# A hybrid DeltaNet and RG-LRU backbone on one core: another formula, buffers and engine split in the RG-LRU scan stage, and layer 1 in column order

## The reference

```python
h_lat = rmsnorm(x, norm_g[i]) * (1.0 + scale[:, None]) + shift[:, None]
if col_major:
    h_lat = to_col_major(h_lat, rows)
...
xb, gate = jnp.split(h @ w_in, [LRU_W], axis=-1)
xc = short_conv(xb, conv_w) + conv_b
r = jax.nn.sigmoid(einsum(xblk, w_r) + b_r)          # per direction, 4 blocks of 256
i = jax.nn.sigmoid(einsum(xblk, w_i) + b_i)
log_a = -RG_C * r * jax.nn.softplus(-lam)
a = jnp.exp(log_a)
b = jnp.sqrt(-jnp.expm1(2.0 * log_a)) * (i * xc)
h_t = a_t * h_{t-1} + b_t                            # forward and backward, from the context's state
y = ((h_f + h_b) * jax.nn.silu(gate)) @ w_out
...
x = x + gate[:, None] * from_col_major(y); return rmsnorm(x, final_g)
```

## Time and profile before

| | us |
|---|---|
| median of 3 runs (4928.4 to 4930.95) | 4929.32 |
| the profiled execution | 4928.78 |
| its span in the trace | 4927.0 |
| norm of layer 1 | 3806 to 3895 |
| projection of layer 1 | to 4304 |
| scan stage: first loads, last product | 4309 to 4727.0 |
| output stage | 4731 to 4927 |

### The profile page before, as it was taken

The page is one execution under the profiler, slowest core; times in us unless marked ns, Lnnn a source line. Parts: engine busy times, 40 slices in busy tenths (PEclk is TensorE's granted clock), DMA queues, the critical chain, the costliest instruction groups (busy, mean ns, idle before and its releaser), DMA issues. The chain is left out here.

```text
span 4927.0 us, 83385 instructions
## 1 busy us (share of the span) xinstructions
PE 4166.3 (85%) x30756; PEld 3449.3 (70%) x30756; DVE 2875.9 (58%) x3373; ACT 2115.1 (43%) x3991; POOL 1906.6 (39%) x1256
## 2 busy tenths in 40 slices
PE   7599999999997888888888888876998599956559
PEld 2378888888885777777777777765887488745447
DVE  3244545454544777777777777765543633268864
ACT  4122222223222666666666666642111611167732
POOL 2212112121211776666666676643110522123222
PEclk8799999999998999999999999997999699978779
DMA  6212221222122444444444444335443221221234
GB/s 230 84 48 78 66 80 54 82 66 77 53 84 75 114 112 114 111 115 114 111 113 111 116 113 114 109 99 197 174 187 118 72 82 57 73 79 62 79 128 141
DMA packets 589103, 503.79 MB, mean 102 GB/s; under 512 B 115585, under 2 KB 557185, under 8 KB 575873
## 3 DMA queue, kind: packets, MB, share of 16 engines
q1 hardware_dynamic: 588960, 501.82, 33.2%
HBM read 351.00 MB, written 150.67 MB: 102 GB/s over the span
## 5 line engine op out<-in xcount | busy, mean ns | idle before, releaser
L551 PE MATMUL pj_bank<-h_hi,pj_whi 128*128 128x512 f32 (+1 forms) x1920 | 717.7, 374 | 22.5 <-POOL pj_wlo L537 19.2
L551 PE MATMUL pj_bank<-h_lo,pj_whi 128*128 128x512 f32 (+1 forms) x1920 | 708.1, 369 | 0.0
L551 PE MATMUL pj_bank<-h_hi,pj_wlo 128*128 128x512 f32 (+1 forms) x1920 | 707.9, 369 | 0.0
L741 ACT ACTIVATE pj_raw<-pj_bank 128x512 f32<-128x512 f32 (+1 forms) x240 | 128.1, 554 | 956.4 <-PE pj_bank L551 477.5
L534 POOL TENSOR_TENSOR pj_whi<-pj_w,ones 128x1024 fp32r<-128x1024 f32 x48 | 115.3, 2403 | 1025.4 <-PE pj_bank L551 1010.9
L551 PEld LDWEIGHTS pj_bank<-h_hi,pj_whi 128*128 128x128 f32 x1920 | 363.3, 189 | 88.1 <-POOL pj_wlo L537 19.6
L1364 DVE TENSOR_TENSOR dc_Y<-dc_psY,dc_pick 128x256 f16<-128x256 f32 x864 | 322.4, 413 | 167.8 <-PE dc_psY L1115 167.8
L1270 ACT ACTIVATE dc_R<-dc_psR 128x256 f16<-128x256 f32 x720 | 245.5, 382 | 394.5 <-PE dc_psR L1131 393.6
L551 PEld LDWEIGHTS pj_bank<-h_lo,pj_whi 128*128 128x128 f32 x1920 | 363.5, 189 | 62.5 <-issue 3.8
L551 PEld LDWEIGHTS pj_bank<-h_hi,pj_wlo 128*128 128x128 f32 x1920 | 363.0, 189 | 61.1
L834 DVE TENSOR_SCALAR pj_acc<-pj_raw,pj_conv_w 128x2307 f32<-128x2307 f32 x32 | 90.7, 2834 | 475.2 <-ACT pj_raw L741 475.2
(11 more groups left out here) (273 smaller groups left out, 10778.2 us busy)
## 6 DMA issues: line engine op xcount, KB each, us to landing
dc_tm<-scratch_tm SPq DMA_DIRECT2D x288, 192.0 KB, 2.4
dc_cgr<-scratch_cgrow SPq DMA_DIRECT2D x288, 128.0 KB, 2.8
dc_fm<-scratch_fm SPq DMA_DIRECT2D x288, 128.0 KB, 2.3
scratch_o<-dc_ob SPq DMA_DIRECT2D x288, 128.0 KB, 2.0
scratch_tm<-pj_tm SPq DMA_DIRECT2D x24, 1152.0 KB, 5.2
pj_w<-in_gdn_w_in SPq DMA_DIRECT2D x48, 512.0 KB, 6.3
scratch_fm<-pj_row SPq DMA_DIRECT2D x16, 1152.0 KB, 5.2
dc_kr<-scratch_fm SPq DMA_DIRECT2D x288, 64.0 KB, 2.6
```

What stands on the lines that cost most here:

```text
L551: i = pe.matmul(self.bank[blk][:, 0:n], l[b][:, k, :], r[:, k, at:at + n], start=(m == 0), stop=(m == 3 * KT - 1))
L741: act.activation(raw_row(raw, blk), pr.bank[blk][:, 0:BLKS[blk][1]], ACT.Silu if KINDS[j] == "z" else ACT.Copy).then_inc(pr.s_ev, 1)
```

## The change

- **Norm of layer 1.** The tiles are taken in column order: a latent tile is four grid columns of 32 tokens, loaded by four DMAs of 32 rows each. Context tiles are loaded by four DMAs as well. `hi` and `lo` are then written contiguously.
- **Formula.** ACT takes `tanh(4z)`, then `a`, then the root of that tanh at once, in the same unit. DVE forms `(1 + a) * root(tanh(4z)) * i * xc`: a product with `xc` (it was POOL's), one with `1 + a`, one with the root. The square of a is gone.
- **Scan in place.** The recurrence writes over its input in `I`, of which there are three; `H` and `V` are gone, and the gate product is written over the gate, contiguously. SP therefore loads a gate only after the store has landed.
- **Second halves.** `whi`, `wlo`, `xhi`, `xlo` have two buffers each and `xc` three rows. ACT and DVE split the next block's first row and weights after unit 0 of a block, the second row after unit 2. All these halves are now ACT's and DVE's; POOL has nothing to do in this stage.
- **PSUM.** The groups are 256, 1024 and 1024 columns a gate, over a ring of four two-bank buffers. PE's code is unrolled.
- **Output stage.** The residual is loaded, and the output stored, by four DMAs of 32 rows a tile each.

The core of the diff:

```diff
@@ phase_norm
-                    sp.dma_start(xt[i % XB][:], src[i * P:(i + 1) * P, :]).then_inc(load[i % XB], 16)
+                    for p, rows in rows_of(i):
+                        sp.dma_start(xt[i % XB][p, :], rows).then_inc(load[i % XB], 16)
...
-                    act.activation(place(hi, i), hsplit(h[i % HB], i), ACT.Copy).then_inc(s_hi, 1)
+                    act.activation(place(hi, i), h[i % HB][:], ACT.Copy).then_inc(s_hi, 1)
...
@@ phase_scan
+    PARTS = [(0, CTX), (CTX, 1024), (CTX + 1024, 1024)]
+    RING = 4
...
-        bank = [ctx.enter_context(nc.psum_tensor(f"sc_b{i}", [P, 512], F32)) for i in range(8)]
+        bank = [ctx.enter_context(nc.psum_tensor(f"sc_b{i}", [P, 1024], F32)) for i in range(RING)]
...
+                            if i >= RING:
+                                pe.wait_ge(s["ev"], i - RING + 1)
...
+                    act.activation(Tn[d][:], A[d][:], ACT.Tanh, scale=c4[:, d, at_row]).then_inc(s["tanh"], 1)
+                    act.wait_ge(s["tanh"], u + 1)
+                    act.activation(A[d][:], A[d][:], ACT.Exp, scale=nc8[:, d, at_row]).then_inc(s["a"], 1)
+                    act.activation(Tn[d][:], Tn[d][:], ACT.Sqrt).then_inc(s["root"], 1)
+                    r = split_after(u)
+                    if r is not None:
+                        x_split(r)
+                        if r % 2 == 0:
+                            w_split(r // 2)
...
+                    dve.tensor_tensor(H[:], H[:], xc[row % XR][:], ALU.mult).then_inc(s["ix"], 1)
+                    dve.wait_ge(s["ix"], u + 1)
+                    dve.wait_ge(s["a"], u + 1)
+                    dve.scalar_tensor_tensor(H[:], A[d][:], 1.0, H[:], ALU.add, ALU.mult).then_inc(s["grown"], 1)
...
+                    dve.wait_ge(s["root"], u + 1)
+                    dve.tensor_tensor(H[:], Tn[d][:], H[:], ALU.mult).then_inc(s["b"], 1)
...
-                dve.tensor_tensor(mixed[:].rearrange("p (r c) -> p c r", c=GRID_W),
-                                  H[0][:, CTX:TOK].rearrange("p (c r) -> p c r", r=ROWS),
-                                  gate[:].rearrange("p (c r) -> p c r", r=ROWS), ALU.mult).then_inc(s["mix"], 1)
+                    dve.tensor_tensor(gate[:], even[:, CTX:TOK], gate[:], ALU.mult).then_inc(s["mix"], 1)
...
@@ phase_output_lru
-                    sp.dma_start(out[bass.ds(at, P), :], y[j][:]).then_inc(stored[j], 16)
+                    dst = columns(out)[bass.ds(at, COLS)]
+                    for c in range(COLS):
+                        sp.dma_start(dst[c], y[j][c * ROWS:(c + 1) * ROWS, :]).then_inc(stored[j], 16)
```

More of the change, by code:

```diff
@@ L175, in phase_norm, with rows_of @@
         ctx_of = lambda i: 1 if i < CCH else 0
[L177 to L186, removed]
+        place = lambda buf, i: buf[:, :, i * P:(i + 1) * P]
+        def rows_of(i):
+            if not col_major:
+                return [(slice(0, P), src[i * P:(i + 1) * P, :])]
+            parts = [slice(c * ROWS, (c + 1) * ROWS) for c in range(COLS)]
+            if i < CCH:
+                return [(p, src[i * P + p.start:i * P + p.stop, :]) for p in parts]
+            latent = src[CTX:TOK, :].rearrange("(r c) d -> c r d", c=GRID_W)
+            return [(p, latent[(i - CCH) * COLS + c]) for c, p in enumerate(parts)]
         def turns(*steps):
@@ L1798, in phase_scan @@
         two = lambda x, s, d=F32: [sb(f"{x}{j}", s, d) for j in range(2)]
[L1799 to L1805, removed]
+        w_raw, wlo = zip(*(raw_under(nc, ctx, f"sc_wlo{j}", [P, 2, 2, 2, 256]) for j in range(2)))
@@ L1806, in phase_scan @@
+        whi = two("whi", [P, 2, 2, 2, 256], F32R)
+        xc = [sb(f"xc{j}", [P, TOK]) for j in range(XR)]
+        xhi, xlo = two("xhi", [P, S2, TOK], F32R), two("xlo", [P, S2, TOK], F32R)
+        gate = sb("gate", [P, SEQ])
+        A, Tn = two("A", [P, TOK]), two("T", [P, TOK])
+        I = [sb(f"I{j}", [P, TOK]) for j in range(3)]
         br, bi = sb("br", [P, 2, KT]), sb("bi", [P, 2, KT])
-        lam, c8, nc8 = sb("lam", [P, 2, KT]), sb("c8", [P, 2, KT]), sb("nc8", [P, 2, KT])
+        lam, c4, nc8 = sb("lam", [P, 2, KT]), sb("c4", [P, 2, KT]), sb("nc8", [P, 2, KT])
@@ L1930, in _ @@
-                root(NU - 1)
+                    at_row = slice(2 * b + t, 2 * b + t + 1)
+                    for g in range(2):
+                        if g == 0 and u >= 2:
+                            act.wait_ge(s["scan"], u - 1)
+                        if g == 1 and u >= 3:
+                            act.wait_ge(s["mix"], (u - 3) // 2 + 1) if u % 2 else act.wait_ge(s["sum"], (u - 4) // 2 + 1)
+                        for n, (at, w) in enumerate(PARTS):
+                            act.wait_ge(s["mm"], u * PER + g * NPART + n + 1)
+                            act.activation((I[u % 3] if g else A[d])[:, at:at + w], bank[(u * PER + g * NPART + n) % RING][:, 0:w],
+                                           ACT.Sigmoid, bias=(bi if g else br)[:, d, at_row]).then_inc(s["ev"], 1)
@@ L1973, in _ @@
-                for u, b, t, d in units:
-                    if u:
-                        scan(u - 1, 1 - d)
-                    dve.wait_ge(s["a"], u + 1)
-                    dve.tensor_tensor(V[:], A[d][:], A[d][:], ALU.mult).then_inc(s["sq"], 1)
-                    dve.wait_ge(s["sq"], u + 1)
-                    dve.wait_ge(s["tanh"], u + 1)
-                    dve.scalar_tensor_tensor(Tn[d][:], V[:], 1.0, Tn[d][:], ALU.add, ALU.mult).then_inc(s["v"], 1)
-                    if u and d == 0:
-                        mix(u // 2 - 1)
-                    if u % 4 == 2 and b + 1 < LB:
-                        split(b + 1)
```

217 lines of the change are left out of this document (108 added, 109 removed).

## The result

| | median, us | lowest to highest | runs | profiled execution | its span |
|---|---|---|---|---|---|
| before | 4929.91 | 4928.4 to 4930.95 | 4 | 4928.78 | 4927.0 |
| after | 4871.59 | 4869.99 to 4877.68 | 4 | 4869.99 | 4868.2 |

The ratio is 0.9884, with a 95% interval of 0.9867 to 0.9901: 1.2% faster, 58 us. The prediction was 4873, with 4855 to 4893 as its own range.

What follows compares the result with a forecast made beforehand. Before, a ring of ACT, DVE and PE bounds the scan stage; after, PSUM's ring between PE and ACT decides. 4928.8 - 42 (scan stage with its start) - 15 (norm) + 1.5 (output) = 4873 us, own range 4855 to 4893.

Steps and rivals of the forecast that it cites:

- a ring of ACT, DVE and PE: Scan stage before: no engine full; ACT waits 54.3 us for DVE, PE 89.5 us for the next block's halves.
- a ring that costs nothing: Scan stage: PE always ahead, ACT's unit 15.3 us, DVE the bound; 4800 us in all, chance 0.04.
- units of 23.5 us: Scan stage: two-bank evictions at 1.4 us and a lasting low clock, 54 us more; 4927 us, chance 0.06.
- A unit of ACT: Scan stage: evictions 9.5 us plus 10.5 of functions and table loads, 20.1 with semaphores, bounds 19.3 and 20.9.
- Half clock when the evictions start: Scan stage: PE stands still 5.5 us in each unit, so its clock falls every unit, staying low until 5 us.
- The price of 2.2 us a unit: Scan stage: what PE's low clock adds to a unit's evictions, making them 9.5 us where full clock gives 7.3.
- The rival with the full clock: Scan stage: PE's clock stays full, a unit takes 17.8 us, stage 37 us shorter still; 4834 us, chance 0.12.
- Hide completely: Scan stage: the next block's split halves stand in second buffers, ready a block ahead, so PE never waits for them.
- The start: Scan stage's beginning: first row's halves are ready, only second row's copy and one subtraction follow; PE starts 5 us sooner.
- It just fits: Layer 1's norm: four DMAs land in 4.3 us, allowing turns of 3.35 us; contiguous hi writes gain 15 us.
- the loads are late in every turn: Layer 1's norm: landing takes 5.5 to 8 us, norm gains 6 or loses 14; 4882 to 4902 us, chance 0.13.
- the rival with SP as the bound: Output stage: nine DMAs a tile instead of three, at 1.8 us each, cost 75 us more; 4948 us, chance 0.05.

Runs made afterwards that it cites:

- the run that holds the clock: Changed kernel plus 21 spare matmuls a unit (30 and 39 after splits) in PE's gap, product overwritten: 4853.9 us, ratio 0.9831.

## Why the prediction came out right, and where its terms were off

The mechanism held stage by stage, as told below. That the time missed by 1.4 us only is in part luck: the forecast gain was 2.8 us too large in the norm, 1.9 too small at the start and 3.9 too small in the scan, the forecast loss in the rest 0.8 too small, and the code ahead of the norm alone moves a total by more than all of these.

**The bound.** The prediction read a ring of ACT, DVE and PE, and said that the change takes DVE out of it and leaves PE and ACT with PSUM between them. The waits after show just that, and the run with eight banks, which alters nothing but PSUM, moves the stage by 53.7 us, while 41 us of DVE's work taken away move it by nothing. The rivals with a ring that costs nothing (DVE would have no idle time) and with units of 23.5 us are out: DVE is busy 263 of 351 us, and units without a copy took 19.4 to 20.3.

**A unit of ACT.** Taken at 20.1 us; after has 19.9 (4341.71 to 4361.64), 19.4 in the unit behind one with a row's copy, 22.2 with such a copy and 23.7 with a copy of weights too. By its sum the stage from first sigmoid to last product is 4684.8 - 4329.9 = 354.9; it measured 351.2. Of the 3.7 us, 2.4 lie in the nine units without a copy, 0.3 us each, and most of the rest in the first unit and in those that also copy weights.

**The clock.** Half clock when the evictions start: right in all 15 units behind the first. It was back 3.6 to 5.8 us after the first sigmoid, where the working took 5. The gap of PE was 5.3 us where it had 5.5; behind a row's copy it was 7.4, behind a row and weights 9.2, which the working left out and which changed nothing, since the clock fell in every one. The price of 2.2 us a unit stands against 1.9 by experiment. The rival with the full clock would have had a stage 37 us shorter, by the units' 2.3 us each; the run that holds the clock shows 29.0 and units of 18.0 (4358.32 to 4376.30, fifth group to fifth group).

**The halves ahead.** "Hide completely" held: no wait of PE for them, and taking them back costs 31.9 us.

**The start.** Gain 6.9 instead of 5. The step said that the second row's copy follows its landing as before, 13.2 us after the stage's first DMA. In the changed kernel it came sooner: the copy begins 4306.85 - 4295.63 = 11.2 us after that DMA. The load is issued 2.5 us after the stage's first DMA (2.0 before), but it is one row and no longer two, and landed 8.7 us after its issue instead of 11.2. Whether its size alone did that wasn't tried.

```profile
4306.85 2.12 ACT L1903 ACTIVATE sc_xhi<-sc_xc 128x2304 fp32r<-128x2304 f32 x1 [1.06 <-DMA sc_xc<-scratch_xc]
```

**The norm.** 12.2 instead of 15, though every `hi` took its 1.04. The load is the mis-sized term. "It just fits" was right for the turns, 3.35 us in most tiles, but the working asked only what the four DMAs do to a turn and put them at nothing for the first tiles, where no turn hides them; there they cost 2.0 us, 2.2 in all. With one DMA the norm gains 98.4 - 84.0 = 14.4. The rival, that the loads are late in every turn, is out: the norm's ACT waited for tokens only 2.9 us beyond the first tile.

```profile
ACT norm_junk L217 <- DMA norm_x<-scratch_tokens: 51.0, 4, 48.1
```

The first tile's wait is 48.1 of the 51.0 us. For that rival the prediction cited the Trainium skill, "SBUF — State Buffer", section "Door 1: The DMA port swizzle", on DMAs that reach 32 partitions. What this case shows is the cost of four such DMAs in place of one: each 128 KB landed 2.7 us after its issue, the 512 KB of the run with one DMA 3.6, and the fourth was issued 1.3 us behind the first. No run tells the ports' part in that from the issues'.

**The output.** Its loop is as long as before, so the loads of `mixed` did come in time, and the rival with SP as the bound is out. (Its price in the prediction is not added up right: by 4.3 x 14 + 18 it is 78, not 75, and nine DMAs at 1.8 us would last 5.3 and not 4.3 us longer than a tile.) The cost is 2.3 instead of 1.5: 1.2 at the very end, where 1.5 had been said, and 1.1 before the loop, which the prediction didn't have. The loop begins 4694.76 - 4665.88 = 28.9 us after the last gate product, 27.8 before. The chain that ended last went through the first load of `mixed`, 4.12 us from issue to landing, and POOL's split of the weights; it now goes through the second load:

```profile
4731.30 4.12 DMA ol_mix<-scratch_mixed
```

```profile
4676.02 14.36 DMA ol_mix<-scratch_mixed
```

That load took 12.6 us before. POOL's split is no quicker a way: it begins 13.1 us after the last store is issued instead of 11.9, because the first load lands after 5.3 us instead of 4.1, and ends 0.15 us ahead of the chain's next step. Why both land later wasn't tried.

**How much each part is worth.** In the scan stage, taking the early split away costs 31.9 us, and adding the contiguous product to the kernel before brings 8.7; together 40.6, beside the 40.9 measured. These are measured in different surroundings and need not add up, but they leave little for the rest. The rest has a gain and a loss in it. ACT's waits for DVE (54.3 us) are gone, and the ring of four large banks takes as much: with eight banks the gain of the stage would have come to 94.6 (392.1 - 297.5), more than twice the 40.9. That the size of the pieces in PSUM ate the difference is shown by that run. Which of the others took ACT's waits away, the new form of the root, the scan in place or POOL's idleness, is not: no run has one of them alone.

## What to carry to other kernels

Where two engines hand over through a ring, count what is left to do when the ring is full, in the columns of the producer at the clock that it will have then: this number, with the rest of ACT's unit, gave the stage to 1%. Before moving a pass from one engine to another, look whether that engine is waited for at all, and in what kernel it is measured: the same step was worth nothing with one ring and 21 us with another. And compare stages, not totals, when executions differ by 12 us in code that no one touched.

## What the runs showed of the hardware

- TensorE's clock was at its lower level (0.50, 1.2 of 2.4 GHz) behind gaps of only 2.4 to 2.6 us in eight of 15 units, and not in the seven others with gaps as long; with gaps of at most 0.6 us it stayed at 1.00 for 15 units. With eight banks it fell behind gaps of 2.1 to 2.2 us as well, in seven of eight units. Filling the gap with matmuls that nobody needs brought 29 us of stage.
- Two-input passes of DVE, scans among them, that meet a two-input pass of POOL wait for its end: 10.22 us for 5.21, 7.54 for 2.56.
- A table load on ACT took 1.28 us in each of its 50 places in the stage after, and the next function began 0.01 us behind it.
- Successive sigmoids from PSUM overlap: those of 512 columns started 0.57 us apart where each shows 0.69, those of 1024 1.00 apart where each shows 1.11.
